# Up and gate projections of a two-block transformer kernel: from single column tiles to pairs of tiles in seven block products

## The chip, the core and the metric

The kernel runs on one NeuronCore of one Trainium2 chip. The metric is the device time of one execution in microseconds (us). Before the change it is 2490.59 us, the median of 3 runs (2489.76 to 2491.76).

The engines are named as in the profile: PE is TensorE (matrix products), PEld its weight loads, DVE is VectorE, ACT is ScalarE, POOL is GpSimd, SP is SyncE, which here only issues transfers.

## The reference

One sequence of 512 tokens with 1024 features passes two blocks, all in float32. The parts that the change touches are the wide layers of the five feed-forward stages (s = 1, 2, 4, 5 and 7):

```
# first block (s = 1), 4096 hidden features
h2 = rms_norm(x, norm_mlp)
x  = x + square(relu(h2 @ w_up)) @ w_down
x  = rms_norm(x, norm_final)
# second block, two layers; feed-forward before (s = 2, 5) and after (s = 4, 7) the mixer, 2816 hidden features
h  = rms_norm_2(x, ffn_norm)
x  = x + 0.5 * ((silu(h @ w_gate) * (h @ w_up)) @ w_down)
```

Around them stand a mixer with two attentions and gates in the first block, and in each layer of the second a mixer with windowed attention and a short convolution. Their computation stays as it is.

## The kernel before

Activations lie transposed: 128 features on the partitions, 512 tokens along the free axis, 8 tiles for 1024 features. A float32 operand is split into two parts of a reduced 32-bit type, hi (a copy rounded to that type) and lo (the rest), and a product is three matmuls: w_hi with h_hi, w_hi with h_lo, w_lo with h_hi (lines 845, 846, 847). One result tile of 128 output features takes 8 k-tiles, so 24 matmuls of 512 columns, into one of four PSUM banks that rotate (`dense`).

A **unit** is the weights of one such tile, 128 x 1024 floats, 512 KB. Three units are held. SP fetches a unit (`fetch`, L1624) as soon as the lo part of the unit three before it is made; ACT makes `w_hi` (L1006), DVE makes `w_lo` in a buffer of its own (L1237). In the mixers' attention parts `w_lo` is instead made by ACT (minus w_hi, L1009) and by a transfer from POOL that adds `w_raw` onto it (L1533).

All engines go through one list of jobs that `Plan` writes out in order. `next_slot` moves a counter after each k-tile of a dense result, and `later(n, job)` puts a job of the other engines at the slot n further on; on each engine the jobs keep the order of that list, so a job that waits holds all jobs behind it on its engine. Every wait is on a semaphore.

A feed-forward stage (`mlp`) alternates. It makes hidden tiles in chunks of 8 (`hidden_tile`: a dense result for `w_up` and, in the second block, one for the gate before it), and then for each of the 8 output tiles one dense result over the chunk's tiles, added to `x` by DVE (`residual`, L1367). In stage 1 DVE takes the result out of PSUM with relu and the norm factor (L1374), ACT squares it (L1109) and makes `act_hi` (L1112), DVE makes `act_lo`. In the others DVE scales (L1229), ACT applies silu (L1117), DVE multiplies gate and up (L1388). The norm factor `rms_inv` is applied after the product, so the first tiles of a stage are multiplied while the sum of squares is made; ACT takes its root (L1045), DVE its reciprocal (L1267).

In the last output tiles before a stage, `norm_tile` makes each tile's `h_hi` (ACT, L1019) and `h_lo` (DVE, L1252) and its square (ACT, L994), which POOL adds up (L1542).

## Time and profile before

| | before |
|---|---|
| median of 3 runs | 2490.59 us (2489.76 to 2491.76) |
| span of the profiled execution | 2488.4 us |
| PE, share of the span | 99% |
| PEld | 82% |
| DVE, ACT, POOL | 50%, 39%, 8% |
| granted TensorE clock, mean of the core | 0.999 |
| moved by DMA | 267.40 MB, mean 107 GB/s |

The profile gives the profiled execution its span, 2488.4 us from the first to the last instruction, and no time beside it. The median of the timed runs is 2.2 us above that span. A share is busy time over the span; a busy time of PE is a union of records that overlap, so the mean of one matmul (some 390 ns for 512 columns) is longer than the distance between two of them. PEld records overlap PE.

### The profile page before, as it was taken

The numbers are of one execution on the slowest core, as the hardware profiler recorded it, in microseconds if no ns is written. First come the engines' busy times: TensorE is split into PE (matmuls) and PEld (weight loads), VectorE is DVE, ScalarE is ACT, GpSimd is POOL, SyncE is SP. The second block draws the span as 40 slices with busy tenths as digits, with TensorE's granted clock in tenths as the row PEclk, the third lists the DMA queues.
The fourth block names the chain that finished last, engine by engine and source line by source line (L and its number), as shares of the span: only waits on it lengthen the run. The fifth ranks groups of instructions, "written<-read, shape, count | busy, mean of one in ns | idle before, by whom it ended". The sixth has DMA issues, their size and how long they took to land.

```text
span 2488.4 us, 27808 instructions
## 1 busy us (share of the span) xinstructions
PE 2471.6 (99%) x11236; PEld 2046.0 (82%) x11236; DVE 1235.0 (50%) x1674; ACT 961.9 (39%) x1415; POOL 198.7 (8%) x207
## 2 busy tenths in 40 slices
PE   9999999999999999999999999999999999999999
PEld 7878888888888888888888888888888888888887
DVE  7742554434474343466554444643444665544443
ACT  6677343322443232357432222422222575322223
POOL 2231010000020000012200000100000122000001
PEclk9999999999999999999999999999999999999999
DMA  7655433333233333245433332333332364333332
GB/s 212 141 129 124 136 102 103 95 100 101 85 94 101 102 93 95 86 134 143 119 94 102 93 101 86 102 95 100 93 102 81 123 142 129 94 102 93 102 91 79
DMA packets 79279, 267.40 MB, mean 107 GB/s; under 512 B 9904, under 2 KB 13232, under 8 KB 78768
## 3 DMA queue, kind: packets, MB, share of 16 engines
q1 hardware_dynamic: 69376, 233.57, 31.0%
q0 software_dynamic: 9776, 32.06, 6.4%
q8 instruction: 89, 1.46, 0.2%
q14 instruction: 38, 0.31, 0.0%
HBM read 234.56 MB, written 2.19 MB: 95 GB/s over the span
## 4 chain that ended last, share of the span: by engine, by line
PE 90%; DVE 3%; issue 2%; ACT 2%; POOL 1%; DMA 1%; SPq 0%; POOLq 0%; DVEq 0%; ACTq 0%
PE bank L845 29%; PE bank L847 29%; PE bank L846 29%; DVE w_lo L1237 1%; PE bank L861 1%; PE bank L876 1%; ACT w_hi L1006 1%; DVE x L1367 1%; PE bank L899 1%; ACT z L994 0%; PE bank L888 0%; PE bank L889 0%; ACT h_hi L1019 0%; POOL rel_bias L1561 0%; POOL square_sum L1542 0%
## 5 line engine op out<-in xcount | busy, mean ns | idle before, releaser
L845 PE MATMUL bank<-h_hi,w_hi 128*128 128x512 f32 x2224 | 872.4, 392 | 3.6 <-DVE w_lo L1237 1.5
L846 PE MATMUL bank<-h_lo,w_hi 128*128 128x512 f32 x2224 | 866.6, 390 | 0.0
L847 PE MATMUL bank<-h_hi,w_lo 128*128 128x512 f32 x2224 | 866.4, 390 | 0.0
L1237 DVE TENSOR_TENSOR w_lo<-w_raw,w_hi 128x1024 fp32r<-128x1024 f32 (+2 forms) x392 | 484.0, 1236 | 289.8 <-ACT w_hi L1006 288.6
L1006 ACT ACTIVATE w_hi<-w_raw 128x1024 fp32r<-128x1024 f32 (+1 forms) x435 | 449.1, 1034 | 398.7 <-PE bank L847 396.5
L845 PEld LDWEIGHTS bank<-h_hi,w_hi 128*128 128x128 f32 x2224 | 417.7, 188 | 88.0 <-DVE h_lo L1252 2.7
L847 PEld LDWEIGHTS bank<-h_hi,w_lo 128*128 128x128 f32 x2224 | 417.5, 188 | 88.0
L846 PEld LDWEIGHTS bank<-h_lo,w_hi 128*128 128x128 f32 x2224 | 417.9, 188 | 81.9 <-issue 0.5
L845 PE MATMUL bank<-act_hi,w_hi 128*128 128x512 f32 x960 | 373.6, 389 | 0.0
L846 PE MATMUL bank<-act_lo,w_hi 128*128 128x512 f32 x960 | 373.6, 389 | 0.0
L847 PE MATMUL bank<-act_hi,w_lo 128*128 128x512 f32 x960 | 373.6, 389 | 0.0
L1229 DVE TENSOR_TENSOR z<-bank,rms_inv 128x512 f32<-128x512 f32 x234 | 163.7, 702 | 285.4 <-PE bank L847 284.1
L1367 DVE SCALAR_TENSOR_TENSOR x<-bank,x 128x512 f32<-128x512 f32 x152 | 104.6, 689 | 282.7 <-PE bank L847 282.7
L1542 POOL TENSOR_TENSOR square_sum<-square_sum,z 128x512 f32<-128x512 f32 x55 | 73.8, 1341 | 1836.3 <-ACT z L994 1836.2
L846 PEld LDWEIGHTS bank<-act_lo,w_hi 128*128 128x128 f32 x960 | 180.2, 188 | 37.5
L845 PEld LDWEIGHTS bank<-act_hi,w_hi 128*128 128x128 f32 x960 | 180.2, 188 | 37.4
L847 PEld LDWEIGHTS bank<-act_hi,w_lo 128*128 128x128 f32 x960 | 180.2, 188 | 37.2
L1122 ACT ACTIVATE act_hi<-z 128x512 fp32r<-128x512 f32 x88 | 55.6, 632 | 384.4 <-DVE z L1388 384.4
L1117 ACT ACTIVATE z<-z 128x512 f32<-128x512 f32 x88 | 55.6, 632 | 286.5 <-DVE z L1229 286.5
L1237 DVE TENSOR_TENSOR act_lo<-z,act_hi 128x512 fp32r<-128x512 f32 x120 | 83.1, 693 | 105.0 <-ACT act_hi L1122 61.4
L1019 ACT ACTIVATE h_hi<-x,gains 128x512 fp32r<-128x512 f32 x56 | 40.5, 724 | 122.4 <-DVE x L1367 119.0
L1533 POOL DMA_DIRECT2D w_lo<-w_raw x51 | 44.7, 877 | 266.1 <-ACT w_lo L1009 262.3
(203 smaller groups left out, 1724.8 us busy)
## 6 DMA issues: line engine op xcount, KB each, us to landing
w_raw<-ffn_wg_dram SPq DMA_DIRECT2D x88, 512.0 KB, 3.5
w_raw<-ffn_wu_dram SPq DMA_DIRECT2D x88, 512.0 KB, 3.5
w_raw<-w_in_dram SPq DMA_DIRECT2D x67, 512.0 KB, 3.6
w_raw<-ffn_wd_dram SPq DMA_DIRECT2D x64, 512.0 KB, 3.5
w_lo<-w_raw POOLq DMA_DIRECT2D x51, 512.0 KB, 4.5
w_raw<-w_up_dram SPq DMA_DIRECT2D x32, 512.0 KB, 3.5
w_raw<-w_down_dram SPq DMA_DIRECT2D x32, 512.0 KB, 3.7
w_raw<-w_out_dram SPq DMA_DIRECT2D x24, 512.0 KB, 3.6
```

Source lines behind the costliest of these rows:

```text
L845: engine.matmul(to, w_hi[s][:, lhs], hi, start=k == 0, stop=False)
L846: engine.matmul(to, w_hi[s][:, lhs], lo, start=False, stop=False)
L847: product = engine.matmul(to, w_lo[s][:, lhs], hi, start=False, stop=job == "k_last")
L1006: engine.activation(w_hi[s][:, 0:width], w_raw[s][:, 0:width], ACT.Copy).then_inc(signals["w_hi"].s, 1)
L1019: engine.activation(h_hi[:, m, :], x[:, m, :], ACT.Copy, scale=h_gain(s, m)).then_inc(signals["h_hi"].s, 1)
L1117: engine.activation(z[zs[1] % Z_RING][:, :], z[zs[0] % Z_RING][:, :], ACT.Silu).then_inc(signals["silued"].s, 1)
L1122: engine.activation(act_hi[:, plan.hidden[key] % FF_RING, :], z[zs[1] % Z_RING][:, :], ACT.Copy).then_inc(signals["act_hi"].s, 1)
L1229: engine.tensor_tensor(to, src, scale, ALU.mult).then_inc(signals["evacuated"].s, 1)
L1237: engine.tensor_tensor(lo, value, hi.bitcast(F32), ALU.subtract).then_inc(signals[event].s, 1)
L1367: engine.scalar_tensor_tensor(x[:, m, :], dense_bank[plan.results[r].bank][:, :], factor(r), x[:, m, :], ALU.mult, ALU.add).then_inc(signa ...
L1533: engine.dma_start(w_lo[s][:, 0:width].bitcast(F32), w_raw[s][:, 0:width], accum_op=ALU.add).then_inc(signals[f"w_added{s}"].s, 16)
L1542: engine.tensor_tensor(to, to, z[zs % Z_RING][:, :], ALU.add).then_inc(signals["scaled_sum" if scaled else "square_sum"].s, 1)
```

## The change

In all five feed-forward stages the up and gate tiles are made in pairs. Such a pair is a **group**: 256 output features by 512 tokens by 1024 input features. Tokens are cut into two halves of 256, output features into the two tiles, and k-tiles into even and odd ones. The group is then seven block products (`PRODUCTS`), each of 4 k-tiles x 3 matmuls of 256 columns, 84 matmuls in place of 48 of 512 columns. There are 16 groups in stage 1 and 22 in each of the others, 104 in all.

**Activation operands.** Besides quarters of h, the products need sums and differences of quarters. `norm_tile` makes them for each pair of k-tiles: ACT makes `h_full` and the plain `h_hi`; DVE makes the four combinations in three instructions (`mix_31`, `mix_2`, `mix_4`), ACT their hi parts, DVE their lo parts two slots later. The lo parts lie in the former `w_lo` buffers.

**Weight operands.** A group's weights (1 MB) lie in seven slots of 128 x 512, held twice (n % 2). SP loads slots B11 and the block that T3 starts from (`s_load_first`, 512 KB), the block that T1 starts from (`s_load_t1`, 256 KB) and B21, B22 (`s_load_last`, 512 KB). POOL issues two transfers of 256 KB from memory that add another block onto T3 and T1. DVE adds T2 = B11 + T3 and T4 = T2 + B21. ACT makes four hi parts (three of 1024 elements a partition, one of 512), DVE four lo parts, in place of the raw weights.

**Results.** P1, P6, P5 and P3 accumulate one after the other in one half bank (x), and ACT copies what stands there after P1, P6 and P5 before the next may add to it. P7 and P4 share another half bank (z) with a copy between. DVE then makes the two output tiles from these copies and the banks.

**Units.** Only down projections and mixers use units now. Where `split_v` makes the lo part, it is written over `w_raw`, and SP fetches the unit three later only when the unit's last matmul is done. Chunks of the 22-tile stages are 6, 8 and 8 tiles (before 8, 8 and 6), and at each chunk's end two further hidden tiles are made ahead (before one).

The core of the diff (new functions of `Plan`, and the parts of the engines' programs that the prediction follows):

```diff
+PRODUCTS = {"P1": (B11, "a11", "x"), "P2": (B21, "a12", "y"), "P3": (B22, "s4", "x"), "P4": (T4, "a22", "z"),
+            "P5": (T1, "s1", "x"), "P6": (T2, "s2", "x"), "P7": (T3, "s3", "z")}
+STEADY = ("P1", "P7", "P6", "P4", "P5", "P2", "P3")
+OPENING = ("P1", "P2", "P4", "P6", "P7", "P5", "P3")
+COPY_AFTER = {"P1": "p1", "P6": "u1", "P5": "u3"}
+COPY_BEFORE = {"P6": "p1", "P5": "u1", "P3": "u3"}
...
+        if s in MLP_STAGES and m % 2 == 1:
+            self.add("h_mix", (s, m // 2))
+            self.later(2, "h_mix_lo", s, m // 2)
...
+    def prepare(self, n):
+        for slots, job, key in ((1, "s_t2", (n,)), (1, "s_hi", (n, "first")), (3, "s_t4", (n,)), (3, "s_lo", (n, "first")),
+                                (5, "s_hi", (n, "mixed")), (5, "s_hi", (n, "last")), (7, "s_lo", (n, "mixed")),
+                                (8, "s_lo", (n, "last")), (9, "s_hi", (n, "t1")), (10, "s_lo", (n, "t1"))):
+            self.later(slots, job, *key)
+
+    def strassen(self, g):
+        if self.prepared == g + 1 and g + 1 < self.block_end:
+            self.prepare(g + 1)
+        for name in group.order:
+            for k in range(HALF_K):
...
+                if k % 2 == 1:
+                    self.next_slot()
+            if name in COPY_AFTER:
+                self.add("s_copy", (g, COPY_AFTER[name]))
+            if name == ("P4" if group.opens else "P7"):
+                self.add("s_copy", (g, "q4" if group.opens else "p7"))
+            if name == "P5":
+                self.add("s_c22_open" if group.opens else "s_c22", g)
+            if name == ("P7" if group.opens else "P2"):
+                self.add("s_sum", g)
+            if name == "P7":
+                self.load_first(g + 2)
+            elif name == "P6" and group.opens:
+                self.norm(self.pending_norm)
+            elif name == "P5":
+                self.load_t1(g + 2)
+                if g + 2 < self.block_end:
+                    self.later(1, "s_add_t3", g + 2)
+                    self.later(6, "s_add_t1", g + 2)
+        self.load_last(g + 2)
...
+        if s == 1:
+            self.strassen(g)
+            self.later(1, "s_relu", g)
+            self.later(1, "s_square", g)
+        else:
+            self.strassen(g)
+            self.later(1, "s_gate", g)
+            self.later(1, "s_silu", g)
+            self.later(4, "s_rescale", g)
+            self.strassen(g + 1)
+            self.later(1, "s_up", g + 1)
+        self.later(2, "s_act", s, pair)
+        self.later(4, "s_act_lo", s, pair)
...
# PE, before a product's first matmul
+                        pe.wait_ge(*done("s_lo", (g, PART_OF[slot])))
+                        if name in COPY_BEFORE:
+                            pe.wait_ge(*done("s_copied", (g, COPY_BEFORE[name])))
# ACT
+                elif job == "s_hi":
+                    if name == "first":
+                        act.wait_ge(s_first_landed[n % 2].s, 16 * (n // 2 + 1))
+                        act.wait_ge(t3_added[n % 2].s, 16 * (n // 2 + 1))
+                    elif name == "mixed":
+                        act.wait_ge(*done("s_t4", n))
+                    else:
+                        act.wait_ge(s_last_landed[n % 2].s, 16 * (n // 2 + 1))
+                    engine.activation(span_of(slot_hi, n, name), span_of(slot_raw, n, name), ACT.Copy)
# DVE
+                elif job == "s_t4":
+                    v.wait_ge(s_last_landed[n % 2].s, 16 * (n // 2 + 1))
+                    v.wait_ge(*done("s_t2", n))
+                    engine.tensor_tensor(slot_raw[:, n % 2, T4, :], slot_raw[:, n % 2, T2, :], slot_raw[:, n % 2, B21, :], ALU.add)
# SP ("s_load_last": last_user is "P3", two blocks)
+                    if n >= 2:
+                        sp.wait_ge(*done("s_mm", (n - 2, last_user)))
...
# SP, fetch of a unit
+                elif u - UNITS_HELD in plan.lo_in_place:
+                    sp.wait_ge(*done("mm_done", plan.unit_result[u - UNITS_HELD]))
```

## Rows read from the trace of the kernel before

**Rows 1.** The page: busy us of each engine, share of the span, instructions.

```profile
PE 2471.6 (99%) x11236; PEld 2046.0 (82%) x11236; DVE 1235.0 (50%) x1674; ACT 961.9 (39%) x1415; POOL 198.7 (8%) x207
```

**Rows 2.** Timeline of DVE in stage 1: start us, length us, instruction, idle before.

```profile
388.38 0.69 DVE L1374 SCALAR_TENSOR_TENSOR z<-bank,rms_inv 128x512 f32<-128x512 f32 x1 [1.21 <-PE bank L847]
...
391.38 1.23 DVE L1237 TENSOR_TENSOR w_lo<-w_raw,w_hi 128x1024 fp32r<-128x1024 f32 x1 [0.26 <-ACT w_hi L1006]
393.82 0.69 DVE L1374 SCALAR_TENSOR_TENSOR z<-bank,rms_inv 128x512 f32<-128x512 f32 x1 [1.21 <-PE bank L847]
```

**Rows 3.** Timeline of PE there: the last matmul of a tile, the first of the next.

```profile
393.32 0.39 PE L847 MATMUL bank<-h_hi,w_lo 128*128 128x512 f32 x1
...
393.55 0.39 PE L845 MATMUL bank<-h_hi,w_hi 128*128 128x512 f32 x1
```

**Rows 4.** Timeline of PE in an attention part.

```profile
46.83 0.28 PE L861 MATMUL bank<-ka_hi,qa 128*128 128x256 f32 x1
46.95 0.28 PE L861 MATMUL bank<-ka_lo,qa 128*128 128x256 f32 x1
47.06 0.40 PE L845 MATMUL bank<-h_hi,w_hi 128*128 128x512 f32 x1
47.30 0.40 PE L846 MATMUL bank<-h_lo,w_hi 128*128 128x512 f32 x1
...
47.76 0.28 PE L861 MATMUL bank<-ka_hi,qa 128*128 128x256 f32 x1
```

**Rows 5.** Timeline of PEld in the same stretch.

```profile
46.84 0.19 PEld L861 LDWEIGHTS bank<-ka_lo,qa 128*128 128x128 f32 x1
46.95 0.19 PEld L845 LDWEIGHTS bank<-h_hi,w_hi 128*128 128x128 f32 x1
```

**Rows 6.** Timeline of PEld right after a wait of PE.

```profile
49.37 0.19 PEld L861 LDWEIGHTS bank<-ka_hi,qa 128*128 128x128 f32 x1 [0.95 <-DVE neg_max L1430]
49.48 0.19 PEld L861 LDWEIGHTS bank<-ka_lo,qa 128*128 128x128 f32 x1
```

**Rows 7.** Groups by line and form: count, busy us, mean ns, idle before.

```profile
L1006 ACT ACTIVATE w_hi<-w_raw 128x1024 fp32r<-128x1024 f32 x403 | 422.8, 1050 | 380.1 <-PE bank L847 377.9 <-DMA w_raw<-w_in_dram 1.8
...
L1133 ACT ACTIVATE probs<-probs,neg_max 128x256 f32<-128x256 f32 x80 | 39.5, 497 | 0.1
...
L1148 ACT ACTIVATE turned_hi<-bank 128x512 fp32r<-128x512 f32 x48 | 28.4, 596 | 49.0 <-PE bank L876 46.1 <-PE bank L889 2.7
```

**Rows 8.** Timeline of ACT in stage 1: two instructions in a row.

```profile
389.76 0.63 ACT L1112 ACTIVATE act_hi<-z 128x512 fp32r<-128x512 f32 x1
390.30 1.05 ACT L1006 ACTIVATE w_hi<-w_raw 128x1024 fp32r<-128x1024 f32 x1
```

**Rows 9.** DMA: queue's packets, MB, share; issues' count, KB each, median us to landing.

```profile
q1 hardware_dynamic: 69376, 233.57, 31.0%
q0 software_dynamic: 9776, 32.06, 6.4%
...
w_raw<-ffn_wg_dram SPq DMA_DIRECT2D x88, 512.0 KB, 3.5
...
w_raw<-w_in_dram SPq DMA_DIRECT2D x67, 512.0 KB, 3.6
...
w_lo<-w_raw POOLq DMA_DIRECT2D x51, 512.0 KB, 4.5
...
w_raw<-ffn_wd_dram SPq DMA_DIRECT2D x32, 384.0 KB, 3.1
```

**Rows 10.** Timeline of PE at the entry to stage 1: last and first matmul.

```profile
354.79 0.39 PE L847 MATMUL bank<-mg_hi,w_lo 128*128 128x512 f32 x1
355.01 0.39 PE L845 MATMUL bank<-h_hi,w_hi 128*128 128x512 f32 x1
```

**Rows 11.** Timeline of DVE at the same entry.

```profile
355.29 0.69 DVE L1367 SCALAR_TENSOR_TENSOR x<-bank,x 128x512 f32<-128x512 f32 x1 [0.97 <-PE bank L847]
356.77 0.75 DVE L1252 SCALAR_TENSOR_TENSOR h_lo<-x,gains,h_hi 128x512 fp32r<-128x512 f32 x1 [0.79 <-ACT h_hi L1019]
```

More of the change, by code:

```diff
@@ L116 @@
     x_before: int | None = None
+@dataclass
+class Group:
+    stage: int
+    kind: str
+    pair: int
+    order: tuple
+    opens: bool
 class Plan:
@@ L134 @@
         "gate": ("gated",), "merge_a": (), "merge_b": ("merged", "mg_hi", "mg_lo"), "residual": (),
-        "relu": ("positive_squared", "act_hi", "act_lo"), "silu": ("silued",), "product": ("product", "act_hi", "act_lo"),
+        "s_c22_open": ("s_c22_part", "s_c22"), "s_step": (), "s_last": ("s_mm",), "s_copy": ("s_copied",), "s_c22": ("s_c22",), "s_sum": ("s_summed",),
+        "s_gate": ("s_out",), "s_up": ("s_out",), "s_relu": ("s_out",), "s_silu": ("silued",), "s_rescale": ("s_scaled",),
+        "s_square": ("s_squared",), "s_act": ("act_hi",), "s_act_lo": ("act_lo",),
+        "s_t2": ("s_t2",), "s_t4": ("s_t4",), "s_hi": ("s_hi",), "s_lo": ("s_lo",),
+        "s_load_first": (), "s_load_t1": (), "s_load_last": (), "s_add_t3": (), "s_add_t1": (),
+        "hs_tile": ("h_full", "h_hi", "h_lo"), "h_mix": ("mix_31", "mix_2", "mix_4", "mix_hi"), "h_mix_lo": ("mix_lo",),
+        "neg_rms": ("neg_rms",),
         "conv_c": (), "conv_h": ("conv_u",), "conv_own": ("conv_own",), "conv_earlier": ("conv_back_1", "conv_back_2"),
@@ L467, in first_mixer, with begin_block @@
         self.pending_norm = 1
+    def begin_block(self, s):
+        n = self.block_end
+        for stage in (s, s + 1) if s + 1 in MLP_STAGES else (s,):
+            if stage == 1:
+                kinds = [("relu", pair) for pair in range(FF1_TILES // 2)]
+            else:
+                kinds = [(kind, pair) for pair in range(FF2_TILES // 2) for kind in ("gate", "up")]
+            for kind, pair in kinds:
+                opens = pair == 0 and kind != "up"
+                self.sg.append(Group(stage, kind, pair, OPENING if opens else STEADY, opens))
+        self.block_end = len(self.sg)
+        self.block_of[n] = s
+        self.block_of[n + 1] = s
+        return n
@@ L494, in mlp @@
         self.phase_result[s] = len(self.results) - 1
-        sizes = [min(FF_CHUNK, n_tiles - start) for start in range(0, n_tiles, FF_CHUNK)]
-        made = 0
+        sizes = CHUNKS_FF[n_tiles]
+        made = start = 0
         for c, size in enumerate(sizes):
-            start = c * FF_CHUNK
-            until = start + size + (c + 1 < len(sizes))
+            last = c == len(sizes) - 1
+            until = n_tiles if last else start + size + 2
             while made < until:
-                self.hidden_tile(s, made)
-                made += 1
-            source, last = ("act", s, start), c == len(sizes) - 1
+                self.hidden_pair(s, made // 2)
+                made += 2
+            if self.prepared <= self.groups_done + 1 and self.prepared < self.block_end:
+                self.prepare(self.prepared)
+            source = ("act", s, start)
             results = self.dense_pair(size, source) if last else []
@@ L1192, in two_blocks @@
         h_until, conv_buffer, merge_result = {}, {}, {}
-        for s in range(1, FINAL):
+        for s in range(1, FINAL + 1):
             h_until[s] = plan.h_last[s - 1]
```

478 lines of the change are left out of this document (366 added, 112 removed).

## The prediction, made before the changed kernel was built

> **What bounds the kernel now.** I read the page first: PE is busy for 99% of the span [rows 1], and a group of 48 matmuls is all that a hidden pair needs. Then the timeline of DVE in stage 1: it takes result tiles out of PSUM every 5.44 us (393.82 - 388.38) [rows 2], which is 24 matmuls 0.227 us apart, so PE never waits for anybody there. DVE idles 1.21 us before each [rows 2]. A hidden pair costs 2 x 5.44 = 10.88 us, and 104 of them 1132 us, nearly half of the span.
>
> **Columns and matmuls.** The change needs 84 x 256 = 21,504 columns where there were 48 x 512 = 24,576, but 36 more matmuls, each with a weight load. It pays for PE if a 256-column matmul starts less than 10.88 / 84 = 0.130 us after the one before. The trace has two such in a row: 46.83, 46.95, 47.06, so 0.115 apart [rows 4]. Lower bound 0.1135 (half of 0.227). Upper bound: the cycle of two short and three long matmuls takes 47.76 - 46.83 = 0.93 us, and 0.93 - 3 x 0.227 = 0.249 leaves 0.124 for each short one. The load record is 0.19 long, which would make 16 us of a group, but the next load starts 0.11 after it [rows 5], so loads overlap. I take 0.118: PE alone needs 9.91 us for a group (9.53 to 10.4), 0.97 less than now.
>
> The Trainium skill, TensorE: Matmul & The Clock Gate, section Back-to-back issue gap, gives a warm gap of columns over 2.4 GHz plus 2.5 ns, so some 109 ns for 256 columns and 216 for 512. By it the group would go from 10.4 to 9.2 us; the rows show 0.227 for the long ones and 0.115 to 0.118 for the short ones, and they decide.
>
> **The other engines' load in a group.** ACT: three hi parts of 1.05, one of 0.63, four copies of 256 columns from PSUM. The copy is not in the trace; between half of 0.596 and 0.497 [rows 7] I take 0.39. With the two or four instructions of 0.63 for silu, square and `act_hi` that is 6.6 to 7.9 us. DVE: three lo parts of 1.23 [rows 2], eight or so of 0.69 and three halves of some 0.42 make 9.8 us end to end, and 8.7 if the 0.08 that neighbours overlap is taken off. So both fit under 9.91, DVE barely. What decides is the order in which they get there.
>
> **The chain that closes on itself.** Follow `s_load_last`. SP issues it for group g+1 when P3 of group g-1 has finished. Group g starts then (time 0). DVE's `s_t4` at slot 3 and ACT's `s_hi` "last" need it. ACT has, in its order: hi "mixed" (needs t4), hi "last", and only behind them the copy u1 that PE needs before P5. P5 has 48 matmuls in front of it in the group, 5.66 us. The steps:
> - last matmul to its consumer: the record of 0.28 plus what lies between record's end and consumer, 393.82 - (393.32 + 0.39) = 0.11 at most [rows 2, 3], less the 0.118 to time 0: 0.2
> - issue to landing of 512 KB: 3.5, or 3.6 where accumulating transfers run in the same part (w_in) [rows 9]; I take 3.6, at 3.8
> - t4 0.69, with a hand-over of 0.03 before and after: 4.55
> - hi mixed and hi last: neighbours on ACT start 0.54 apart when one takes 0.63 [rows 8], so 1.05 counts as 0.96: 6.47
> - copy u1 0.39: 6.86
> - PE's restart with an exposed weight load of 0.11 [rows 6] and a hand-over: 0.17, P5 starts at 7.03, 1.37 after 5.66.
> - P5, P2, P3: 36 x 0.118 = 4.25: P3 ends at 11.28, and starts the next load.
>
> So a steady group takes 11.3 us whatever PE's columns cost: 0.4 more than before. DVE and ACT have slack inside it, so no other step adds. Bounds: 3.4 to land, 0.1135 a matmul and 0.3 for the copy give 10.8; an accumulating transfer that holds up the load gives more (rival 2). In stage 1 the squares and `s_act` stand before it on ACT (out 0.65, two squares 1.87, hi first 2.8, copy p1 3.1 against P6's 2.83), which gives a smaller stall at P6 that the same chain takes in. 85 of the 104 groups are steady: 104 less 5 openings, 11 firsts behind a down projection, 3 at the end of a block. 85 x 0.4 = +34 us.
>
> **First group behind a down projection.** It prepares no weights, but the last unit's split is in its first slot. As lo lies over raw, SP fetches only when the unit's matmuls are done (before: from the lo part on, 5 us earlier), and ACT's w_hi stands in front of copy p1: 0.2 + 3.6 + 0.03 + 0.96 + 0.39 + 0.17 = 5.35 against P6's 2.83, so 2.5 lost: 9.91 + 2.5 - 10.88 = +1.5, 11 times +17. Within the down projections the same fetch costs nothing: hi and lo are ready 0.2 + 3.6 + 1.05 + 1.23 = 6.1 after it, needed after two more tiles, 8.2 or 10.9.
>
> **Openings.** Before, PE goes from the last output tile to the stage without a gap [rows 10], and the last h_lo is there at 357.52, 2.25 before its first matmul at 355.01 + 21 x 0.227 = 359.77 [rows 11]. Now the last two tiles also need mixes before P6, 45 matmuls or 5.3 us in: x at 0.9, `h_full` 1.65, `h_hi` 2.3, h_lo 3.0, three mixes in a row to 4.8, ACT's wide hi 5.7, then w_hi 6.6 and DVE's w_lo 7.9 and t2 in front of `h_mix_lo` (0.42 and 0.96), 9.7, PE at 9.9. Stall 4.6 less the 0.97 of columns: +3.6; with the last residual up to 0.8 late because w_lo now ends 6.1 after the tile before, +4.4. Five: +22. Lower bound 0 if the tail is hidden, upper 8 each.
>
> **Ends of blocks.** The 3 last groups prepare nothing: -0.97 each, -3.
>
> **Sum.** +34 +17 +22 -3 = +70. Made against the span of 2488.4, which lies 2.2 below the median; I carry the difference over: 2490.6 + 70, rounded to 2562.
>
> **Rivals.**
> 1. *Columns decide after all.* If `s_load_last` lands before P7 ends, or ACT gets to u1 in time, PE runs at 9.91: 104 x -0.97 = -101, openings +15, 2405. For it: ACT and DVE have the capacity. Against it: it needs the chain 1.4 us shorter, and the load alone is 3.5, with 2.83 of P1 and P7 before t4's slot. A half of it, a chain of 10.5 with cheap openings, gives 2460.
> 2. *The accumulating transfer lies on the load.* `s_load_t1` is issued after P5, 2.83 before the end, lands about 0.1 after it, and POOL's transfer then moves its bytes while `s_load_last` moves its own. The software queue takes 6.4% of 16 engines for 32 MB, 5.0 us a MB, so 1.24 for 256 KB [rows 9]. If all of it delays the load, the group takes 12.5: 85 x 1.6 = +136, with the rest 2665. For it: the times meet. Against it: w_in loads land only 0.1 later than others where such transfers run. The Trainium skill (Trainium Kernel Development and Optimization, Key Constraints) says that transfers issued from SP and POOL run on the same 16 engines and interleave; by it the 1.24 would fall in part on the load; no row here shows the two overlapping.
> 3. *The chain is as short as its lower bound*, 10.8, and the entries cost little: within 0.2% of before, 2490.
>
> That DVE becomes the bound (9.8 end to end) changes nothing while the chain is 11.3.
>
> **Chances.** Forecast 0.60, with its own range 2520 to 2620; rival 1 0.14 and its half 0.08; rival 2 0.12; rival 3 0.06. A change under 0.2% can't be told from none here. Faster 0.23, same 0.05, slower 0.72. The range of 2450 to 2650 leaves out rival 1 (0.14) and about half of rival 2.
>
> **What would show it.** In the changed profile PE must wait once in each steady group, before P5, for ACT's copy of u1, by about 1.4 us, and P1 of one group to P1 of the next must be 11.3. ACT's hi "mixed" must start right behind `s_t4`, and `s_t4` right behind the landing of `s_load_last`. Matmuls of 256 columns should start 0.118 apart. First groups behind a down projection should wait about 2.5 before P6 for copy p1, with ACT waiting for a landing. Openings should wait before the last k-tile of P6 for the lo of the mixes. PE's busy share should fall from 99% to about 90%. I am wrong if the groups are under 10.5, or if the wait is before P1 or P7 and names DVE.

## The result, and the profile after

| | before | changed |
|---|---|---|
| time, median (before: run again on the same chip) | 2490.71 us | 2821.62 us (4 runs, 2802.12 to 2826.0) |
| ratio | | 1.1312, interval 1.1275 to 1.1348 |
| span of the profiled execution | 2488.4 us | 2824.2 us |
| granted TensorE clock, mean | 0.999 | 0.961 |
| moved by DMA | 267.40 MB | 345.65 MB |

The change makes the kernel 13% slower. The forecast was 2562 us with a range to 2650: the direction was right, the size far off.

The page of the changed kernel: busy us, share of the span, instructions, against [rows 1].

```profile
PE 2514.8 (89%) x14980; PEld 2238.8 (79%) x14980; DVE 1683.2 (60%) x2520; ACT 1285.8 (46%) x2111; POOL 371.5 (13%) x407
```

No engine is full. PE is busy for 43 us longer, and in a span that is 336 longer. Its waits follow, with DVE's and ACT's that feed them. The columns are total us, times, longest.

```profile
PE bank L1074 <- ACT part_a L1293: 198.6, 150, 5.8
...
ACT slot_hi L1278 <- DVE slot_raw L1574: 158.0, 94, 3.3
...
DVE slot_raw L1574 <- DMA slot_raw<-ffn_wu_dram: 103.7, 41, 3.9
DVE slot_raw L1574 <- DMA slot_raw<-ffn_wg_dram: 100.1, 39, 3.7
...
PE bank L1074 <- DVE h_lo L1514: 32.8, 10, 4.9
PE bank L1046 <- DVE w_raw_lo L1514: 30.5, 9, 6.5
```

The first four lines are the closed chain as forecast: landing of `s_load_last`, t4 (L1574), wide hi parts (L1278), copy into `part_a` (L1293), P5. Both p1 and u1 are written to `part_a`, so the 150 waits are of two kinds: 77 of them, 103 us, lie before P5 in a steady group, and the other 73 before a P6. The last two lines are the openings and the output tiles ahead of them. The DMA lines (packets, MB, share; KB each, median us to landing) answer to [rows 9]:

```profile
q1 hardware_dynamic: 84352, 260.84, 30.5%
q0 software_dynamic: 38576, 82.40, 17.1%
...
slot_raw<-ffn_wg_dram SPq DMA_DIRECT2D x88, 512.0 KB, 4.7
slot_raw<-ffn_wu_dram SPq DMA_DIRECT2D x88, 512.0 KB, 4.5
...
w_raw<-ffn_wd_dram SPq DMA_DIRECT2D x64, 512.0 KB, 3.5
slot_raw<-ffn_wg_dram POOLq DMA_DIRECT2D x88, 256.0 KB, 5.2
```

A load of 512 KB still lands in 3.5 in the down projections (`w_raw`), but in 4.5 to 4.7 into the slots. These medians take `s_load_first` and `s_load_last` together; `s_load_last` alone, the one in the chain, has a median of 4.4. The 5.2 takes the transfers onto T3 and T1 together; over all 104 groups those onto T3 have 4.3 and those onto T1 5.5.

**Where the 336 us lie.** From the starts of PE's matmuls each group has a length (first matmul to the first one of what follows) and seven stretches, one for each product in the order of `OPENING` or `STEADY`; 1.44 is a product without a wait. The fourth of a steady group is that of P4 and ends where P5 starts. The table gives means in us. "Follower" is the second group of a stage. The last column is the sum of (length - 10.88), so the loss against the 48 matmuls of before.

| changed kernel | groups | length | stretches in running order | over before |
|---|---|---|---|---|
| opening | 5 | 26.76 | 6.26 5.11 4.60 4.40 1.97 2.89 1.53 | +79 |
| follower | 5 | 17.54 | 1.44 6.85 2.70 2.20 1.48 1.44 1.44 | +33 |
| steady | 80 | 12.45 | 1.44 1.96 1.51 2.91 1.60 1.58 1.45 | +126 |
| behind a down projection | 11 | 13.44 | 1.43 3.93 1.96 1.78 1.46 1.44 1.44 | +28 |
| end of a block | 3 | 10.08 | seven times 1.44 | -2 |
| outside groups | | 1428.3, before 1356.9 | | +71 |

The sum is 264 + 71 = 336, as the spans differ by 335.8. The forecast had +34 for 85 steady groups (the 5 followers counted among them), 17 behind a down projection, 22 for openings, -3 for ends, and nothing outside.

**A steady group that goes as forecast, and one that doesn't.** Timeline of the changed kernel; one group starts at 426.06, another at 1090.35, a third at 1447.91, the group behind a down projection at 1077.73.

```profile
429.82 0.69 DVE L1574 TENSOR_TENSOR slot_raw<-slot_raw 128x512 f32<-128x512 f32 x1 [2.32 <-DMA slot_raw<-w_up_dram]
430.55 2.01 ACT L1278 ACTIVATE slot_hi<-slot_raw 128x1024 fp32r<-128x1024 f32 x2
432.47 0.36 ACT L1293 ACTIVATE part_a<-bank 128x256 f32<-128x256 f32 x1
432.97 0.36 PE L1074 MATMUL bank<-hs_hi,slot_hi 128*128 128x256 f32 x1 [0.41 <-ACT part_a L1293]
...
1081.61 1.06 ACT L1234 ACTIVATE w_hi<-w_raw 128x1024 fp32r<-128x1024 f32 x1 [4.63 <-DMA w_raw<-ffn_wd_dram]
1082.58 0.37 ACT L1293 ACTIVATE part_a<-bank 128x256 f32<-128x256 f32 x1
...
1095.32 0.69 DVE L1574 TENSOR_TENSOR slot_raw<-slot_raw 128x512 f32<-128x512 f32 x1 [3.52 <-DMA slot_raw<-ffn_wg_dram]
1098.47 0.36 PE L1074 MATMUL bank<-hs_hi,slot_hi 128*128 128x256 f32 x1 [1.61 <-ACT part_a L1293]
...
1456.45 0.36 PE L1074 MATMUL bank<-hs_hi,slot_hi 128*128 128x256 f32 x1 [2.61 <-ACT part_a L1293]
1456.64 0.28 PE L1075 MATMUL bank<-w_lo,slot_hi 128*128 128x256 f32 x1
1456.76 0.38 PE L1076 MATMUL bank<-hs_hi,slot_lo 128*128 128x256 f32 x1
1456.93 0.41 PE L1074 MATMUL bank<-hs_hi,slot_hi 128*128 128x256 f32 x1
1457.14 0.41 PE L1075 MATMUL bank<-w_lo,slot_hi 128*128 128x256 f32 x1
```

The same third group beside one that starts at 1594.09, as stretches (us; busy us and instructions of PE, PEld, DVE, ACT, POOL; granted clock; DMA share; GB/s):

```profile
1594.09:1606.99 12.90, 10.52 (x87) 10.18 (x86) 8.97 (x14) 6.55 (x11) 1.76 (x2) 1.00 0.69 164
1447.91:1462.31 14.40, 11.79 (x86) 11.61 (x85) 9.02 (x14) 4.99 (x9) 1.14 (x3) 0.88 0.53 129
```

In the first group t4 starts 3.76 after its beginning (forecast 3.8), the copy 6.41 (forecast 6.47), P5 6.91 (forecast 7.03), and the group takes 11.30 (forecast 11.28). In the second t4 starts at 4.97, because the load landed 1.2 later, and the group takes 12.50. In the third PE waits 2.61 in all, and then its matmuls start 0.21 apart instead of 0.12: the lower of the two clock levels, half of 2.4 GHz. That group takes 14.40.

All 80 steady groups fall into line by the landing of `s_load_last`. In 24 of them it lands in under 3.75, and they take 11.33 in the mean, as forecast. The other 56 have a later landing and take more. The 65 groups at the upper clock level have a mean landing of 4.2 and take 12.0; the 15 that ran partly at the lower level have 5.3 and take 14.4. The clock's own part shows where landings are alike: the groups at 1594.09 and 1447.91 have 5.15 and 5.17, start P5 8.51 and 8.54 in, and take 12.90 and 14.40, so 1.5 for the clock. A landing of 3.6 everywhere would take 65 us out of the 94 that 80 groups lie above 11.28; some 22 of the other 29 are 15 times 1.5 (an estimate from this pair; the groups behind a down projection differ by 1.5 too, 14.1 against 12.6). So the pattern of 11.3 is the floor of a steady group, not its mean.

### The profile page after: what moved, and what is told of

It is laid out like the page before. It is cut to its first block, busy times and chain, and to the rows that moved or that the text cites. A ratio compares the mean times of both kernels' runs of the same rounds, so it can differ in the third digit from the quotient of the medians.

```text
span 2824.2 us, 37784 instructions
## 1 busy us (share of the span) xinstructions
PE 2514.8 (89%) x14980; PEld 2238.8 (79%) x14980; DVE 1683.2 (60%) x2520; ACT 1285.8 (46%) x2111; POOL 371.5 (13%) x407
## 2 busy tenths in 40 slices
DMA packets 123103, 345.65 MB, mean 122 GB/s; under 512 B 14768, under 2 KB 18096, under 8 KB 122544
## 4 chain that ended last, share of the span: by engine, by line
PE 57%; DMA 17%; ACT 11%; DVE 10%; issue 5%; POOL 0%; SPq 0%; ACTq 0%; DVEq 0%; POOLq 0%
PE bank L1046 11%; PE bank L1047 11%; PE bank L1048 11%; PE bank L1074 7%; DMA slot_raw<-ffn_wg_dram 6%; PE bank L1076 6%; PE bank L1075 6%; ACT slot_hi L1278 5%; DMA slot_raw<-ffn_wu_dram 5%; DVE slot_raw L1574 2%; DMA w_raw<-ffn_wd_dram 2%; DMA slot_raw<-w_up_dram 1%; ACT w_hi L1234 1%; DMA w_raw<-w_out_dram 1%; ACT part_a L1293 1%
## 5 line engine op out<-in xcount | busy, mean ns | idle before, releaser
L1074 PE MATMUL bank<-hs_hi,slot_hi 128*128 128x256 f32 x1248 | 377.3, 302 | 202.9 <-ACT part_a L1293 198.6
L1074 PE MATMUL bank<-h_hi,slot_hi 128*128 128x256 f32 x1664 | 489.3, 294 | 39.6 <-DVE h_lo L1514 32.8
L1278 ACT ACTIVATE slot_hi<-slot_raw 128x1024 fp32r<-128x1024 f32 (+1 forms) x416 | 382.6, 944 | 263.3 <-DVE slot_raw L1574 158.0
L1075 PE MATMUL bank<-h_lo,slot_hi 128*128 128x256 f32 x1664 | 486.0, 292 | 0.0
L1076 PE MATMUL bank<-h_hi,slot_lo 128*128 128x256 f32 x1664 | 484.8, 291 | 0.0
L1514 DVE TENSOR_TENSOR slot_lo<-slot_raw,slot_hi 128x1024 fp32r<-128x1024 f32 (+1 forms) x416 | 443.0, 1084 | 1.8 <-ACT slot_hi L1278 1.8
L1048 PE MATMUL bank<-act_hi,w_raw_lo 128*128 128x512 f32 x960 | 377.9, 394 | 0.0
L1076 PE MATMUL bank<-hs_hi,slot_lo 128*128 128x256 f32 x1248 | 364.9, 292 | 0.0
L1046 PE MATMUL bank<-h_hi,w_hi 128*128 128x512 f32 x560 | 224.7, 401 | 5.0 <-DMA w_lo<-w_raw 3.8
L1047 PE MATMUL bank<-h_lo,w_hi 128*128 128x512 f32 x560 | 219.5, 392 | 0.0
```

Of the source, the lines that this page charges most:

```text
L1046: engine.matmul(to, w_hi[s][:, lhs], hi, start=k == 0, stop=False)
L1047: engine.matmul(to, w_hi[s][:, lhs], lo, start=False, stop=False)
L1048: product = engine.matmul(to, unit_lo(u)[:, lhs], hi, start=False, stop=job == "k_last")
L1074: engine.matmul(to, slot_hi[:, g % 2, slot, lhs], hi, start=opens, stop=False, skip_group_check=True)
L1075: engine.matmul(to, slot_hi[:, g % 2, slot, lhs], lo, start=False, stop=False, skip_group_check=True)
L1076: product = engine.matmul(to, slot_lo[:, g % 2, slot, lhs], hi, start=False, stop=closes, skip_group_check=True)
```

## The experiments

All are timed in three rounds with a kernel before on the same chip (2491.6, 2490.4, 2490.6 and 2489.6 us in the four series). The changed kernel is the base unless another is named. "Steady" is the mean over 80 groups as above.

### Series 1: the chain

```diff
 e1
-  (5, "s_hi", (n, "mixed")), (5, "s_hi", (n, "last"))
+  (6, "s_hi", (n, "mixed")), (6, "s_hi", (n, "last"))
 e2: e1 and
-  (1, "s_hi", (n, "first"))
+  (2, "s_hi", (n, "first"))
```

> The changed kernel with the hi parts mixed and last one slot later, so that on ScalarE they stand behind the copy u1. Chain theory: in a steady group the stretch from P4's to P5's start, now 2.8 us in the mean, falls to about 1.5, since the landing of the last load no longer stands before that copy; some 85 groups times 1.2 us, so 2820 falls to about 2710. Capacity theory (VectorE or the transfers are simply full): the wait moves to another product of the same group and the time stays at 2800 to 2830.

> As the one before, and the hi part first also one slot later, behind the copy p1. Chain theory: the stretch from P7's to P6's start falls from 1.95 to 1.44 us in groups that follow a relu or gate group (about 50), 25 us more, so about 2685; first groups behind a down projection keep their wait of 2.5 us, since that is for the landing of a unit. Capacity theory: no change against the run before.

e1 took 2752.9 us (ratio 1.104, 1.1018 to 1.1061): 69 less by one slot on ACT, where some 110 were expected. The wait before P5 is gone (P4's stretch 2.91 to 1.59), steady 11.62, median 10.88; a part comes back before P6 (P7's stretch 2.53), where copy p1 stands behind hi "first". e2 moves that too: 2721.8 (1.0927), steady 11.38. The order of ACT's instructions closed the chain, as the prediction had it.

```diff
 e3 (accumulating transfers on one partition: most of the two sums is left out)
-  engine.dma_start(slot_raw[:, n % 2, slot, :], group_source(n)[:, block_, :], accum_op=ALU.add)
+  engine.dma_start(slot_raw[0:1, n % 2, slot, :], group_source(n)[0:1, block_, :], accum_op=ALU.add)
 e5
   if job == "s_add_t1":
+      pool.wait_ge(s_last_landed[n % 2].s, 16 * (n // 2 + 1))
```

> The changed kernel with both accumulating transfers cut to one partition (2 KB in place of 256 KB), so nearly all of the two weight sums is left out. Contention theory: the 512 KB loads of the slots land in 3.5 us again, in place of 4.6, and steady groups lose 1.1 us each: about 2725. If the landing is late for another reason (two loads in flight, instruction fetches), it stays at 4.6 and the time within 1% of 2820.

> The changed kernel with one wait more on GpSimd: the transfer that adds onto T1 is issued only when the last load of the same group has landed. Contention theory: the 512 KB loads land in some 3.6 to 4.0 us in place of 4.6, steady groups fall from 12.45 to 11.7 or less, the time from 2820 to 2740 to 2770. If it is the other accumulating transfer (onto T3, beside the first load) that delays, nothing moves: the median landing may fall, but not the group.

e3 took 2735.3 (1.098), e5 2758.9 (1.1078). Loads of 512 KB in e5, where all bytes are still moved but T1's no longer beside this load:

```profile
slot_raw<-ffn_wg_dram SPq DMA_DIRECT2D x88, 512.0 KB, 3.6
slot_raw<-ffn_wu_dram SPq DMA_DIRECT2D x88, 512.0 KB, 3.6
slot_raw<-ffn_wg_dram POOLq DMA_DIRECT2D x88, 256.0 KB, 4.7
```

In e3 they land in 3.6 too. So it is T1's accumulating transfer that lies on the load, by about 1 us; steady falls to 11.49 and 11.69. That is the prediction's rival 2. The Trainium skill (Trainium Kernel Development and Optimization, Key Constraints: transfers of SP and POOL run on the same 16 engines and interleave) agrees with it. T1's own landing gains too when they are apart (median from 5.5 to 4.7). With the transfer held back no steady group ran at the lower clock level either, so the 63 us of e5 are landings and clock together.

```diff
 e4, on the kernel before
   elif plan.lo_by[u - UNITS_HELD] == "w_lo_v":
       sp.wait_ge(*done("w_lo_v", u - UNITS_HELD))
+      sp.wait_ge(*done("mm_done", plan.unit_result[u - UNITS_HELD]))
```

> The kernel before, with only the fetch of the changed one: where the lo part is made by VectorE, a unit is fetched only when the unit three before it has finished its matmuls. My prediction: nothing in the down and hidden tiles, since the parts are ready 6.1 us after the fetch and needed after 10.9; at most 10 us in all (2491 to 2501). Rival: VectorE and ScalarE, in order, wait for landings in front of other work, and out projections and mixers lose what the changed kernel lost outside of its groups in the mixers, some 30 us or more (2520).

e4 took 2520.1 (1.0117, 1.0101 to 1.0133), 28 to 29 more. Between the tiles of the hidden chunks and within the inner down projections nothing is lost. The loss lies where a tile of 8 k-tiles is followed by work of ACT and DVE: in the last chunk before a norm (an eight-tile chunk 47.4 instead of 43.3) and in the mixers and out projections. This is a price of the change that the prediction called nothing.

### Series 2: the openings

```diff
 e6
-  self.add("h_mix", (s, m // 2));  self.later(2, "h_mix_lo", s, m // 2)
+  m < KT - 1:  self.later(2, "h_mix", ...);  self.later(9, "h_mix_lo", ...)
+  else:        self.add("h_mix", ...);       self.later(1, "h_mix_lo", ...)
 e7: e2, e5 and e6 together
 e8 (the mixes are left out, the products read plain halves in their place)
-  self.add("h_mix", ...);  self.later(2, "h_mix_lo", ...)
```

> The changed kernel with the mixes of h (but the last pair's) two slots later, behind the next unit's split, and their lo parts nine slots later, behind the next tile's residual. Entry theory (VectorE and ScalarE, in order, hand each other one step at a time in front of a feed-forward stage, 16.4 us for two output tiles that take TensorE 10.9): the last output tiles before a stage are no longer late, the openings fall from 26.8 by 4 to 8 us each, in all 30 to 60 us less: about 2775. Rival (the pair's tail alone makes the openings long): under 10 us.

> All four orders together: hi parts mixed, last and first one slot later, the T1 transfer after the last load, the mixes spread. If the effects add: 2722 less 30 to 60 for the entries and 10 to 40 for the landings, about 2640; still slower than before, because openings, firsts behind a down projection and the second group of a stage stay long. Rival (VectorE, at about 9.8 us of work a group, is now the bound): steady groups stay at 11.4 and the time above 2680.

> The changed kernel without the mixes of h at all (the products take plain quarters in their place, so the sums of the activations are left out of the computation). Entry theory: the mixes and what queues behind them cost 60 to 110 us in all, so 2710 to 2760, with openings near 18 us in place of 26.8. Rival (openings are long because of the norm's root and reciprocal and the first groups' weights): openings stay over 23 us and the time over 2790.

e6 took 2795.5 (1.1222, where 30 to 60 us less were expected), e7 2751.6 (1.104), e8 2722.1 (1.094). The mixes cost about 99 us, 9 in each opening (26.8 to 17.9) and the rest ahead of it and in fewer groups at the lower clock. Spreading them gains 26, and not in the openings, which stay at 27.4.

e7 is worse than e2, which was not expected. Timeline of ACT and PE in e7:

```profile
868.28 0.63 ACT L1282 ACTIVATE slot_hi<-slot_raw 128x512 fp32r<-128x512 f32 x1 [2.08 <-DMA slot_raw<-ffn_wu_dram]
868.82 0.36 ACT L1297 ACTIVATE part_b<-bank 128x256 f32<-128x256 f32 x1
869.23 0.39 PE L1078 MATMUL bank<-hs_hi,slot_hi 128*128 128x256 f32 x1 [0.93 <-ACT part_b L1297]
```

ACT now waits 2.08 for T1's transfer, which e5 put behind the load, and copy u3, which P3 needs, stands behind that hi part. One closed chain was cut and the next one closed: load, transfer, hi "t1", u3, P3 (P2's stretch 2.70, steady 11.87).

### Series 3: chains cut, and GpSimd's part

```diff
 e9 (the norm's sums are left out but for two columns)
-  engine.tensor_tensor(to, to, z[zs % Z_RING][:, :], ALU.add)
+  engine.tensor_tensor(to[:, 0:2], to[:, 0:2], z[zs % Z_RING][:, 0:2], ALU.add)
 e10: e2, e5 and
-  (9, "s_hi", (n, "t1")), (10, "s_lo", (n, "t1"))
+  (11, "s_hi", (n, "t1")), (12, "s_lo", (n, "t1"))
 e11: e10, e6 and, for the last tile of an inner down projection,
-  self.dense(size, 0, source)
+  self.dense(size, 0, source, slots=7)
 e12: e10, the last edit of e11, e3, e8 and e9
```

> Question: is DVE slowed at the entries by the additions that POOL makes there? POOL adds up the squares of the norm on two columns instead of 512 (the norm's sums are left out of the computation). In the changed kernel the three-part mix takes 1.78 us beside POOL's 1.34 us addition against 1.61 elsewhere, and w_raw_lo up to 2.08 against 1.22. Theory (POOL slows DVE): w_raw_lo is back at 1.22 to 1.25 in the last output tiles, the widest mix at 1.61, and the last two output tiles' cycle of 16.4 us loses 1.5 to 2.5: 20 cycles, 30 to 50 us less, 2770 to 2790 in all. Rival (DVE is held by ACT and by its own order, the slow instructions lie where it would wait anyway): w_raw_lo is at 1.22, and the time falls by under 10.

> Question: when both closed chains are cut at once, does the steady group come down to the columns? e2 (copies before the wide hi parts) with the T1 transfer issued only once the last load has landed, as in e5, and ACT's hi part of T1 at slot 11, behind copy u3, instead of 9 (its lo part at 12 instead of 10). In e7 PE waited 1.2 us before P3 for copy u3, which stood behind that hi part. Theory (two chains, nothing else): P3's wait vanishes, the 512 KB loads land in 3.6, steady groups take 10.4 to 10.9 (e2: 11.38, e7: 11.87), 80 of them save 40 to 75 against e2's 2722: 2650 to 2685. Rival (the whole schedule is one ring: DVE and ACT are within 1 to 2 us of the period, and any delay comes out elsewhere): steady 11.2 to 11.5, total 2700 to 2725.

> Question: how much of the loss can be had back by orders alone? e10 with the mixes of h two slots and their lo parts nine slots on (only the last pair at once), as in e6, and the split of the last unit of a down projection seven slots on, behind the copies of the next group. Theory for the last: the group behind a down projection, 13.4 in the changed kernel of which 2.5 before P6 is for copy p1 behind that split, comes down to 10.9 or less, 11 times 2.5 = 27. The mixes: e6 gave 26 on the changed kernel. So e10 less 30 to 50. Rival: the delayed split delays the next fetch or the next copy as much as it frees, and the post group stays over 12.8; then e10 less 0 to 20. In either case it stays slower than the kernel before, by 110 or more, because the entries and the late fetch remain.

> Question: are the named costs all there are? e10 with everything that was found left out of it: no mixes of h, accumulating transfers on one partition, square sums on two columns, and the last unit's split behind the next group's copies. The mixes, the sums of weights and the norm's sums are missing from the computation. Theory (nothing unnamed is left): steady groups 10.1 to 10.4 as the bare ones of 10.08, the group behind a down projection under 10.9, openings under 15; with 104 groups 60 to 75 under before's 1132, openings and followers 40 to 60 over, the late fetch of the units +28 (e4): 2480 to 2530. Rival (a cost without a name, for instance DVE as the bound by its 9.8 us end to end): steady over 10.8, total over 2570.

| | time | ratio, interval | opening | follower | steady | behind down | outside |
|---|---|---|---|---|---|---|---|
| changed | 2821.6 | 1.1312, 1.1275 to 1.1348 | 26.8 | 17.5 | 12.45 | 13.4 | 1428.3 |
| e9 | 2764.6 | 1.1103, 1.1071 to 1.1135 | 24.4 | 17.7 | 12.01 | 13.0 | 1409.6 |
| e10 | 2670.2 | 1.0729, 1.0703 to 1.0756 | 26.3 | 16.3 | 10.74 | 12.7 | 1424.0 |
| e11 | 2637.2 | 1.0586, 1.057 to 1.0602 | 25.6 | 16.1 | 10.78 | 10.07 | 1419.6 |
| e12 | 2526.9 | 1.0144, 1.0129 to 1.0159 | 15.4 | 15.5 | 10.53 | 10.07 | 1384.2 |

e10: with the T1 transfer behind the load and each copy ahead of the hi part that waits for a landing, a steady group is below the 10.88 of before. Four hi parts moved on ACT (with one lo part on DVE) and one transfer held back give 151 us back, all of it in the groups' waits (1395.9 to 1243.7 in all groups). e11: the group behind a down projection is bare (10.07) once the split stands behind the copies, which is 29 of the 32 us between the traces of e10 and e11. Spreading the mixes, worth 26 in e6, brought almost nothing here. e12: with every named cost left out the groups take 1139 us (before 1132) and the rest lies 27.3 above before, about what e4 gives for the late fetch. Openings and followers are still 46 us over in it, and the openings take 15.4, where under 15 were expected. The steady groups take 10.53, where 10.1 to 10.4 were expected: 0.45 above a bare one, 36 us in all that no run gives a name to.

e9 is the surprise. The additions are in nobody's path, and yet 57 us go with them, where 30 to 50 were expected. The mean ns of a mix (L1544) and of `w_raw_lo` on DVE, first in the changed kernel:

```profile
L1514 DVE TENSOR_TENSOR w_raw_lo<-w_raw,w_hi 128x1024 fp32r<-128x1024 f32 x152 | 191.9, 1263 | 363.4 <-ACT w_hi L1234 363.1
...
L1544 DVE TENSOR_TENSOR h_mixed<-h_full 128x512 f32<-128x512 f32 x20 | 32.1, 1607 | 0.0
```

and in e9:

```profile
L1514 DVE TENSOR_TENSOR w_raw_lo<-w_raw,w_hi 128x1024 fp32r<-128x1024 f32 x152 | 186.6, 1228 | 361.3 <-ACT w_hi L1234 361.1
...
L1544 DVE TENSOR_TENSOR h_mixed<-h_full 128x512 f32<-128x512 f32 x20 | 13.7, 685 | 0.0
```

The timeline of the changed kernel ahead of stage 2 shows how:

```profile
768.02 1.28 POOL L1922 TENSOR_TENSOR square_sum<-square_sum,z 128x512 f32<-128x512 f32 x1 [4.64 <-ACT z L1222]
769.26 1.28 POOL L1922 TENSOR_TENSOR scaled_sum<-scaled_sum,z 128x512 f32<-128x512 f32 x1
769.54 2.08 DVE L1514 TENSOR_TENSOR w_raw_lo<-w_raw,w_hi 128x1024 fp32r<-128x1024 f32 x1 [1.58 <-ACT w_hi L1234]
771.55 0.68 DVE L1763 SCALAR_TENSOR_TENSOR x<-bank,x 128x512 f32<-128x512 f32 x1
...
774.19 1.34 POOL L1922 TENSOR_TENSOR square_sum<-square_sum,z 128x512 f32<-128x512 f32 x1 [3.65 <-ACT z L1222]
774.31 1.78 DVE L1544 TENSOR_TENSOR h_mixed<-h_full 128x512 f32<-128x512 f32 x1
```

GpSimd's addition ends at 775.53, and 0.68 later, at 776.09 to 776.21, the mix is done, as if DVE had not worked until GpSimd was through. In the same way 770.54 + 1.22 = 771.76 against the 771.62 at which `w_raw_lo` ends. The Trainium skill (SBUF — State Buffer, Who interferes with whom) says that a VectorE instruction with two inputs from SBUF contends with a GpSimd instruction that reads SBUF, and that this contention is an exclusive lock. This case's rows agree: in the changed kernel the 17 mixes that ran beside an addition took 1.77 in the mean, and the 3 others 0.68. The prediction has no term for it.

But 35 of the 70 us between the two profiled executions lay in steady groups, where GpSimd adds nothing; there 5 groups instead of 15 ran partly at the lower clock level. Series 4 asks for both.

### Series 4: the sums and the clock

```diff
 e13: e11, and for the feed-forward stages DVE adds instead of GpSimd
+  self.add("square_own", ...);  self.later(2, "square_add", s, m)
+  elif job == "square_add": engine.tensor_tensor(square_sum[:, :], square_sum[:, :], z[...][:, :], ALU.add)   # DVE
 e14: e11 and e9
 e15: e11, and ahead of the k-tile's first matmul
+  if group.opens and name in ("P1", "P2") and k == HALF_K - 1:
+      for _ in range(32):
+          engine.matmul(value_bank[:, first_half], ones_r[:, :], slot_hi[:, g % 2, slot, 0:TOKENS // 2], start=True, stop=True)
```

> Question: is it GpSimd's access beside DVE that costs, or the work? e11 with the additions of the norm's squares made by DVE, two slots after the tile, in place of GpSimd (same computation). Theory (GpSimd beside DVE slows DVE): each addition costs DVE 0.69, seven an entry, 4.8 us, but the four mixes an entry get back to 0.69 from 1.61 and the w_raw_lo from up to 2.3 to 1.22, together 6 to 7 us: net gain of a few us an entry, 0 to 25 in all against e11's 2637, 2612 to 2637. Rival (DVE's time is what lacks): 24 to 40 more, 2660 to 2680.

> Question: the bound for e13. e11 with GpSimd's additions of squares on two columns (the norm's sums are missing). In the changed kernel this gave 57. Of these 36 lay in the steady groups, where GpSimd adds nothing: I take those for fewer groups at the lower clock level, which e11 hasn't any of among its steady groups. Theory: 20 to 35 less than e11, 2602 to 2617, steady groups at 10.8 as before. Rival (the additions cost the steady groups too): 40 or more less.

> Question: is the lower clock behind the stalls of the openings a cost of its own? e11 with 32 matmuls of 256 columns (3.8 us at 0.118) into a bank that nobody needs, before the last k-tile of P1 and of P2 in each of the 5 opening groups, where TensorE waits 4.2 and 4.4 us for h_lo. In e11 the matmuls behind such a wait start 0.213 apart. Theory (idle time brings the clock down): the group's matmuls start 0.118 apart, the 15.6 + 8.9 us lost that way in openings and followers fall by half or more, and the time by 5 to 15: 2622 to 2632. Rival 1 (the waits of ACT and DVE set the openings' length, the clock is hidden in them): distances come down and the time stays within 3 of 2637. Rival 2 (the clock falls for another reason): distances stay 0.213 and the time rises by 5 to 20, as the fill runs at the lower clock too and ends behind the wait.

e13 took 2628.65 (1.0564, 1.0548 to 1.0581), and nothing is left out. Its median is 8.5 below e11's, but the two intervals overlap: shown is that DVE can do 24 us of additions more (35 of 0.68) without a loss, as its mixes fall from 1115 ns in e11 to 738; a gain is not shown. It has the lowest median of the versions that leave nothing out, and is still 5.6% behind the kernel before. e14 took 2606.4 (1.0468), 31 less than e11, with the steady groups as in e11 (10.81): 31 is what the additions cost by themselves. The other 26 of e9's gain go with its fewer steady groups at the lower level; that the additions set those off is not shown.

e15 took 2631.8 (1.0567, 1.0549 to 1.0585), 5.4 less than e11. PE behind the first long wait of stage 2's opening, in e11:

```profile
753.39 0.58 PE L1078 MATMUL bank<-h_hi,slot_hi 128*128 128x256 f32 x1 [4.24 <-DVE h_lo L1518]
753.77 0.42 PE L1079 MATMUL bank<-h_lo,slot_hi 128*128 128x256 f32 x1
753.99 0.41 PE L1080 MATMUL bank<-h_hi,slot_lo 128*128 128x256 f32 x1
```

and in e15:

```profile
747.57 4.00 PE L1075 MATMUL bank<-slot_hi,ones_r 128*128 128x256 f32 x32
752.00 0.38 PE L1081 MATMUL bank<-h_hi,slot_hi 128*128 128x256 f32 x1 [0.43 <-DVE h_lo L1521]
752.22 0.28 PE L1082 MATMUL bank<-h_lo,slot_hi 128*128 128x256 f32 x1
752.34 0.28 PE L1083 MATMUL bank<-h_hi,slot_lo 128*128 128x256 f32 x1
...
764.50 0.39 PE L1081 MATMUL bank<-hs_hi,slot_hi 128*128 128x256 f32 x1 [3.04 <-ACT part_a L1300]
```

The matmuls behind the wait are 0.12 apart instead of 0.21. The stretch from 748 to 768 (busy us and instructions of PE, PEld, DVE, ACT, POOL; granted clock; DMA share; GB/s) in e11:

```profile
748.00:768.00 20.00, 9.82 (x46) 8.86 (x44) 13.38 (x17) 9.13 (x16) 6.55 (x5) 0.61 0.07 20
```

and in e15:

```profile
748.00:768.00 20.00, 13.63 (x102) 12.82 (x102) 12.18 (x16) 9.24 (x17) 5.22 (x5) 0.95 0.05 18
```

So filling the idle time kept the clock up in this stretch (0.61 to 0.95). But the wait for `part_a` grows from 1.51 to 3.04, and the openings as a whole are not shorter (26.35 against 25.62). The time of 2631.8 lies in the range of the theory (2622 to 2632) and outside that of rival 1 (within 3 of 2637), yet the 5.4 us lie outside the openings and the two intervals overlap, so the time decides nothing. The lengths speak for rival 1: in an opening ACT and DVE set the time, and the lower clock is hidden behind them. The fill did not reach everywhere: of the distances at the lower level, 163 in the openings fell to 78, and 96 in the followers to 84. In the steady groups of the changed kernel the clock is not hidden (1.5 us a group, by the pair of groups above).

## Why the prediction was wrong

Measured were 331 us more, forecast 70, with 2650 as the upper end of the range. Four steps failed: the openings and what stands ahead of them, the landing of the load in the chain, the late fetch that was put at nothing, and the clock that had no term.

**Columns: right.** Matmuls of 256 columns start 0.120 apart (median of 8795 pairs; forecast 0.118), and a bare group takes 10.08 (forecast 9.91). ACT's copy takes 0.36 to 0.38 (forecast 0.39).

**The chain: right in every link, wrong in one size.** "I take 3.6, at 3.8" is the term that failed. The load lands in 3.6 when nothing lies on it, and then the group takes 11.30. In 56 of 80 groups it landed later, mostly in 4.1 to 5.4, and the mean group takes 12.45. That is rival 2's number, partly by luck: rival 2 has no clock in it, and the groups at the upper level take 12.0. I gave that rival 0.12, because `w_in` loads land only 0.1 later in the part where accumulating transfers run [rows 9]; those transfers just don't meet them in time. I had worked out that here they do. e3 and e5 show it: landing 3.6 again. Nor had the sum a term for the clock: 15 steady groups ran partly at the lower level, at 1.5 each some 22 of the 94 us of excess; the late landings make 65 of it. Steady groups: forecast +32 for these 80, measured +126; e10 removes it all by order and one transfer held back.

**"Within the down projections the same fetch costs nothing": wrong by 28.** It holds for the inner ones, and the step did not look at the last chunk, the out projections and the mixers, where ACT and DVE are not free when the late unit lands (e4's 28 to 29; e12's rest of 27.3 agrees).

**First group behind a down projection: right.** ACT waits for the landing, w_hi, then the copy, in the rows at 1081.61; P6 starts at 1083.08 after 2.33 of waiting (forecast 2.5), and that group takes 12.6, forecast 12.4. Six of eleven fell to the lower clock behind it and took 14.1, so that the eleven cost 28 where 17 were forecast. e11 takes the wait away with one slot number.

**Openings: the step that failed most.** Forecast 15.3 and measured 26.8, a follower of 17.5 that was not foreseen at all, and some 43 us (71 less the 28 of the fetch) in the output tiles ahead. The step timed one tile's tail from the last `residual`, with each instruction at its length from before. It missed that all four pairs of tiles need mixes, so that DVE and ACT fall behind from tile to tile: two output tiles ahead of stage 2 take 16.4 (`residual` at 755.08 and 771.55) where PE needs 10.9. It missed that GpSimd's additions block the mixes (1.61 instead of 0.69), 31 us in e14. And it stopped at P6, so that the followers were not seen. Their wait is before P6 too, for copy p1. The norm's reciprocal (3.35 on DVE) stands before the opening's first sums, ACT's silus or squares wait for what DVE makes of these, and p1 stands behind them; in the changed kernel it also stands behind hi "first", which in stage 2 waits for the transfer onto T3:

```profile
803.35 3.35 DVE L1673 RECIPROCAL rms_inv<-z 128x512 f32<-128x512 f32 x1 [0.70 <-ACT z L1346]
...
814.17 1.06 ACT L1278 ACTIVATE slot_hi<-slot_raw 128x1024 fp32r<-128x1024 f32 x1 [3.17 <-DMA slot_raw<-ffn_wg_dram]
...
815.64 0.55 PE L1074 MATMUL bank<-hs_hi,slot_hi 128*128 128x256 f32 x1 [5.83 <-ACT part_a L1293]
```

With hi "first" behind p1 (e2, e10) followers fall from 17.5 to 16.2 and 16.3. The rest of this account is read from rows; no run leaves the reciprocal out. e8 puts the mixes at 99, e12 leaves 46 for openings and followers without them.

**The clock: not in the forecast.** At the lower level 86 matmuls of 512 columns and 728 of a group ran, and by their distances that is 84 us (17 and 67); before 0.4 for the long ones. The page of before shows 0.999 with PE busy for 99%, which says nothing of what a wait does to the clock. The granted clock in the stretch ahead of and into stage 2:

```profile
755.00:775.00 20.00, 16.21 (x57) 12.80 (x58) 11.67 (x15) 9.74 (x15) 5.94 (x5) 0.83 0.14 39
775.00:795.00 20.00, 10.46 (x52) 9.04 (x51) 11.45 (x14) 9.89 (x16) 6.17 (x6) 0.82 0.10 33
```

(columns: busy us and instructions of PE, PEld, DVE, ACT, POOL; clock; DMA share; GB/s). How much of the 84 is a cost of its own can't be read from the distances: in the openings it is hidden as far as e15 shows, in steady groups it lengthens the ring by 1.5 us each.

**Sums.** 2490.6 + 70 is 2561, not 2562. DVE's pieces add up to 10.5 with eight instructions of 0.69 (9.8 is with seven); measured are 9.0 to 9.3 us of busy DVE in a steady group. Neither changes the outcome.

**The signs named beforehand.** One wait a steady group before P5 for u1: yes, in 77 of 80. "About 1.4": 1.47 on average (2.91 - 1.44), with 0.5 before P6 on top, in 52 groups. hi "mixed" behind t4, t4 behind the landing: yes. P6 waiting for copy p1 behind a landing: yes, 2.5. PE at 90%: 89%. Openings waiting in P6 for the lo of the mixes: hardly, 0.32 in the first opening; the long waits, up to 4.9, are at the last k-tile of P1 and of P2, for `h_lo` of the last tiles.

**What stays open.** Why a steady group falls to the lower level in one run and not in another (15, 17, 9, 0, 5 and 0 of them in the changed kernel, e1, e2, e5, e9 and e10) was not settled. The length of a wait alone does not decide it: in the changed kernel one group fell behind a wait of 1.75 us, its longest (at 1847.93), and another stayed at 1.00 behind one of 2.70 (at 1495.31). Whether openings can be made cheap was not tried past e15: the rows suggest a second `part_a` and fewer mixes rather than an order, and no run shows it. As the bare groups would save 83 us and the late fetch, the mixes and the openings cost more, no version beat the kernel before.

## What to carry to other kernels

Where PE is at 99%, saved columns only count if the new feeding chain is shorter than the product it feeds: write each loop "landing, combine, round, copy, product, next load" as a ring and compare it with the bare period, with the landing at what it takes beside every other transfer issued in the same microsecond. On an engine that works in order, put what TensorE waits for ahead of what waits for memory; four hi parts moved and one transfer held back were worth 151 of the 331 us here. And give waits of a few microseconds on TensorE a term for the clock, and instructions of VectorE with both operands in SBUF a term for GpSimd work that runs beside them.

## What the runs showed of the hardware

- An accumulating transfer of 256 KB from memory (onto T1) took 5.5 us to land when issued beside a plain load of 512 KB, and 4.7 when issued behind it (e5). The load of the same group took 4.4 and 3.6 (medians of 104).
- GpSimd's addition of 128x512 floats (1.3 us) lengthens a `TENSOR_TENSOR` of DVE with both operands in SBUF as if it held it back until it ends (0.69 becomes 1.78, 1.22 becomes 2.08). Three additions of DVE with one operand in PSUM (`x<-bank,x`) ran beside it in 0.68, as without it. The same seven additions an entry, made by DVE itself, cost no more in all (e13).
- The clock fell to the lower level behind a wait of 2.61 us in a group that was busy otherwise (1456.45), and stayed at the upper behind one of 2.70 in another (1495.31). It stayed up behind the first long wait of stage 2's opening when that was filled with matmuls that nobody needs (e15).
